# Strassen-like feed-forward tiles: the raw weight blocks fetched from ScalarE's queue instead of GpSimd's

## The reference

```
def _swiglu(x, w_gate, w_up, w_down):
    return (jax.nn.silu(x @ w_gate) * (x @ w_up)) @ w_down
```

## Time and profile before

| | before |
|---|---|
| median of 3 runs | 2195.53 us |
| profiled execution | 2196.21 us |
| its span | 2194.5 us |
| PE busy | 2070.7 us (94%) |
| DVE, ACT, POOL busy | 1491.7, 1085.4, 936.0 us |
| TensorE clock granted, mean | 0.991 of full speed |
| GpSimd's queue of transfers | 20096 packets, 72.18 MB |
| ScalarE's queue | 11712 packets, 27.27 MB |
| SP's queue | 51120 packets, 182.08 MB |

### The profile page before, as it was taken

The page is one execution under the profiler, slowest core; times in us unless marked ns, Lnnn a source line. Parts: engine busy times, 40 slices in busy tenths (PEclk is TensorE's granted clock), DMA queues, the critical chain, the costliest instruction groups (busy, mean ns, idle before and its releaser), DMA issues.

```text
span 2194.5 us, 34752 instructions
## 1 busy us (share of the span) xinstructions
PE 2070.7 (94%) x11738; PEld 1799.7 (82%) x11738; DVE 1491.7 (68%) x2525; ACT 1085.4 (49%) x1982; POOL 936.0 (43%) x709
## 2 busy tenths in 40 slices
PE   8999999898899989888999999999999998988998
PEld 6878888698888879888887788888878887988886
DVE  5597854787752378886258789899777348877523
ACT  4566653544442354444244476777655334444422
POOL 2233451755643275664327701201264317565431
PEclk9999999999999999999999999999999999999999
DMA  5322263455533244554325422222454434555321
GB/s 169 113 91 94 77 221 91 149 173 173 179 126 96 77 153 156 176 177 133 96 86 163 124 68 82 77 78 82 134 173 158 154 96 136 184 178 176 121 96 67
DMA packets 83026, 282.78 MB, mean 129 GB/s; under 512 B 9224, under 2 KB 9480, under 8 KB 82416
## 3 DMA queue, kind: packets, MB, share of 16 engines
q1 hardware_dynamic: 51120, 182.08, 26.5%
q0 software_dynamic: 20096, 72.18, 9.7%
q10 hardware_dynamic: 11712, 27.27, 3.3%
HBM read 261.03 MB, written 18.89 MB: 128 GB/s over the span
## 4 chain that ended last, share of the span: by engine, by line
PE 56%; issue 15%; DVE 12%; POOL 11%; ACT 2%; DMA 2%; POOLq 1%; SPq 0%; DVEq 0%; ACTq 0%
PE bank L188 15%; PE bank L190 15%; PE bank L189 15%; PE bank L195 2%; PE bank L194 2%; DMA w_raw<-stream 2%; DVE w_lo L162 2%; POOL s_raw L809 2%; POOL s_holes L812 2%; POOL s_raw L810 2%; POOL s_raw L812 2%; POOL s_holes L809 1%; PE bank L2218 1%; POOL s_holes L810 1%; DVE t_lo L666 1%
## 5 line engine op out<-in xcount | busy, mean ns | idle before, releaser
L162 DVE TENSOR_TENSOR w_lo<-w_raw,w_hi 128x1024 fp32r<-128x1024 f32 (+1 forms) x337 | 455.6, 1367 | 335.5 <-ACT w_hi L157 332.8
L157 ACT ACTIVATE w_hi<-w_raw 128x1024 fp32r<-128x1024 f32 (+1 forms) x337 | 331.2, 985 | 391.0 <-PE bank L190 233.0
L188 PE MATMUL bank<-xn_hi,w_hi 128*128 128x512 f32 (+1 forms) x1192 | 434.2, 364 | 7.5 <-DVE h L662 4.1
L190 PE MATMUL bank<-xn_hi,w_lo 128*128 128x512 f32 (+1 forms) x1192 | 419.8, 352 | 0.0
L189 PE MATMUL bank<-xn_lo,w_hi 128*128 128x512 f32 (+1 forms) x1192 | 418.8, 351 | 0.0
L188 PEld LDWEIGHTS bank<-xn_hi,w_hi 128*128 128x128 f32 x1192 | 226.1, 190 | 38.9 <-DVE h L662 5.4
L190 PEld LDWEIGHTS bank<-xn_hi,w_lo 128*128 128x128 f32 x1192 | 225.5, 189 | 31.0
L189 PEld LDWEIGHTS bank<-xn_lo,w_hi 128*128 128x128 f32 x1192 | 226.1, 190 | 28.2 <-issue 2.6
L843 POOL TENSOR_TENSOR down_lo<-h,down_hi 128x512 fp32r<-128x512 f32 x66 | 112.4, 1708 | 239.7 <-ACT down_hi L603 239.7
L188 PE MATMUL bank<-down_hi,w_hi 128*128 128x512 f32 x528 | 206.4, 391 | 6.3 <-POOL down_lo L843 6.3
L190 PE MATMUL bank<-down_hi,w_lo 128*128 128x512 f32 x528 | 206.2, 390 | 0.0
(11 more groups left out here) (488 smaller groups left out, 4933.0 us busy)
## 6 DMA issues: line engine op xcount, KB each, us to landing
w_raw<-stream SPq DMA_DIRECT2D x337, 512.0 KB, 3.6
s_raw<-stream POOLq DMA_DIRECT2D x54, 512.0 KB, 4.6
s_holes<-stream POOLq DMA_DIRECT2D x48, 512.0 KB, 4.9
spill_g<-gate_out ACTq DMA_DIRECT2D x16, 256.0 KB, 2.0
m_more<-spill_g POOLq DMA_DIRECT2D x3, 1024.0 KB, 11.1
s_first<-stream POOLq DMA_DIRECT2D x6, 512.0 KB, 4.3
x<-xt SPq DMA_DIRECT2D x4, 512.0 KB, 7.3
x<-xt ACTq DMA_DIRECT2D x1, 2048.0 KB, 9.7
```

The lines of the kernel that those rows point to most:

```text
L157: nc.scalar.activation(w_hi[:, slot, at], w_raw[:, slot % 2, at], ACT.Copy).then_inc(split_hi, 1)
L162: nc.vector.tensor_tensor(w_lo[:, slot, at], w_raw[:, slot % 2, at], w_hi[:, slot, at], ALU.subtract).then_inc(split_lo, 1)
L188: nc.tensor.matmul(to, a_hi, b_hi, start=start, stop=False, skip_group_check=True)
L190: return nc.tensor.matmul(to, a_lo, b_hi, start=False, stop=stop, skip_group_check=True)
```

## The change

The raw fetches move from GpSimd's list to ScalarE's. The first one stands after the root of the norm, the second in the third plain tile. Then `third_raw` stands ahead of the first `seven` and behind each `seven` up to the 15th: it waits for the fourth low part of the tile after this one, and issues the two transfers of the tile three ahead into the same buffer. GpSimd's `sums` wait for a landing and nothing else. The transfers count on two semaphores of their own. The loop of ScalarE ends one pass earlier, and that pass is written out. What the transfers carry, their sizes, their buffers and all sums and low parts stay as they were.

```diff
+        raw_in = x_in[2:]
...
+            def raw_to(eng, i, q):
+                for g in range(2):
+                    chunk = stream[4 * i + (first_in + gate_of(q) + g)]
+                    if q == 0 or (isinstance(i, int) and i == 0):
+                        to = (s_raw if q == 0 else s_first)[:, g].rearrange("p h w -> p (h w)")
+                        eng.dma_start(to, chunk).then_inc(raw_in[q], 16)
+                    else:
+                        eng.dma_start(s_holes[g][:, :, H:S], chunk.rearrange("p (k c) -> p k c", c=H)
+                                      ).then_inc(raw_in[q], 16)
...
                                      scale=1.0 / D).then_inc(m["root"], 1)
+                raw_to(act, 0, 0)
...
+                def third_raw(i, q):
+                    of, to = {-1: ((i, 0), (i + 1, 0)), 0: ((i, 1), (i + 1, 1)), 1: ((i + 1, 0), (i + 2, 0))}[q]
+                    act.wait_ge(c["lo"], part_made("lo", *of, 4))
+                    raw_to(act, *to)
...
+                    if t == 2:
+                        raw_to(act, 0, 1)
                     silu_of(t % 2, 2 * t + 2 * b + 1)
+                third_raw(0, -1)
                 for q in range(2):
                     seven(0, q, True)
-                with act.Fori(1, BODIES - 1) as i:
+                    third_raw(0, q)
+                with act.Fori(1, BODIES - 2) as i:
                     for q in range(2):
                         seven(i, q, True)
+                        third_raw(i, q)
+                for q in range(2):
+                    seven(BODIES - 2, q, True)
+                    if q == 0:
+                        third_raw(BODIES - 2, q)
...
-                def next_raw(i, q):
-                    pool.wait_ge(c["lo"], part_made("lo", i, q, 4))
-                    raw_to(i + 1, q)
-
                 def sums(i, q):
-                    pool.wait_ge(gates_in[q], 32 * i + (raw_loaded[q] + 32))
+                    pool.wait_ge(raw_in[q], 32 * i + (raw_loaded + 32))
...
-                raw_to(0, 1)
-                sums(0, 0)
-                sums(0, 1)
-                finished(pool, first_in, 2 * PLAIN - 1)
-                for q in range(2):
-                    next_raw(0, q)
-                    sums(1, q)
-                with pool.Fori(1, BODIES - 1) as i:
+                for i in range(2):
                     for q in range(2):
-                        next_raw(i, q)
-                        sums(i + 1, q)
+                        sums(i, q)
+                with pool.Fori(2, BODIES) as i:
+                    for q in range(2):
+                        sums(i, q)
```

## The result

The changed kernel takes 2251.84 us (median of four runs, 2250.97 to 2254.33), the kernel before 2195.61 beside it: a ratio of 1.0258, 95% interval 1.0241 to 1.0276. The change makes the kernel 56 us slower. I had forecast slower, by 18.7 us, and the range ended at 2240. The profiled run of the change took 2250.97 us.

The account below looks back on a forecast made before the run. GpSimd's ring of issue, landing and sums was taken to pace the kernel at 11.76 us a tile. A new ring of 12.25 gave 606.5 against 587.8, +18.7 on 2196.2, less 0.7: 2214 us, range 2150 to 2240.

Parts of the forecast that it names:

- (1): GpSimd in the loop: issuing and waiting, 5.06 us per tile, leave it; four sums remain, so it is no bound.
- (2): ScalarE's wait for S3's low part stands ahead of snap 0, which TensorE's S2 block needs; that closes a new ring.
- the 10.4: Length in us of a tile in the new ring without any hindrance from GpSimd's sums, 0.3 over the matmuls.
- Step (3): In the loop GpSimd's sums and vector operations take turns: a tile is L + 7.27, 12.25 us in the mean, against 11.76.
- step (5): Ahead of the loop: GpSimd's first sums come earlier, ScalarE's second fetch late; taken as zero, bounds -2 and +2 per feed-forward.
- L: Time from the end of S3's low part until the fetched blocks are there: 4.7 us for s_raw, 5.2 for s_holes.
- The turn of 0.42: Time in us added when a GpSimd sum and a two-operand vector operation exclude each other; three counted per tile.
- Step (4): The count: 15 tiles of 12.25 plus 18.4 for the last two intervals, 202.2 per feed-forward; +18.7 us over three.
- The ring goes and nothing takes its place: Rival: GpSimd's ring leaves the loop and no sum is in the way; 10.4 us a tile, 2136 us; chance 0.27 with its half-hindered case.
- its half-hindered case: Rival's variant: half the turns fall into the vector engine's idle time; 11.2 us a tile, 2169 us; within the shared 0.27.
- The tie: Rival: quicker landing (L = 4.3) or luckier turns make old and new rings equal; 11.75 us a tile, 2192 us; chance 0.16.
- The slow queue: Rival: transfers are slower on ScalarE's queue, L = 5.5; 12.8 us a tile, 2239 us; chance 0.12.

Follow-up runs that it names:

- small sums: The changed kernel with each of GpSimd's four sums on 16 of 512 columns; 2141.31 us, ratio 0.9755.
- the wait in the kernel before: The kernel before with only ScalarE's wait for S3's low part added behind each silu, GpSimd still issuing; 2229.91 us, ratio 1.0136.
- the wait kept at the old place: The changed kernel with ScalarE's issues moved behind snap 0 of the next tile, its wait also kept ahead of the weights' high part; 2247.92 us.
- s_raw's single transfer: The changed kernel with the two transfers of each even tile (s_raw) made one of 1024 KB; 2243.58 us, ratio 1.0222.

## Why the prediction came out as it did

**The mechanism was right.** Steps (1) and (2): GpSimd is busy 87.5 of 194 us of the loop (below) and bounds nothing; snap 0 behind S3's low part closes a ring, and TensorE's largest wait is the one forecast, 2.1 us for snap 0. The price of that ring without turns was low: ScalarE needs 1.70 us (573.81 to 575.51) or 1.52 (586.93 to 588.45) before the high part, where I put 0.95. That turns the 10.4 into 11.1, what the small sums measured.

**Step (3) failed in size.** 12.25 us a tile predicted, 13.13 measured in the first feed-forward (441.79 to 638.68, 15 intervals); 0.88 x 45 = 40 us, of a miss of 38; the last two intervals added 1 and step (5), below, gave back 5; the last 2 are the rounding of the forecast and the median against the profiled run. Each tile splits at its first sum, at L. Means over the first feed-forward:

| | predicted | measured |
|---|---|---|
| L, block in s_raw | 4.7 | 5.15 (4.83 to 5.31) |
| L, block in s_holes | 5.2 | 5.94 (5.80 to 6.27) |
| from the first sum on | 7.27 | 7.28 to 7.30 where the turns go as walked; 7.55 in the mean |

L is 0.62 longer, 28 of the 40 us. The queue isn't slower. Issues of the stretch 485 to 640, answering to the earlier trace rows (count, KB, median us from issue to landing):

```profile
s_holes<-stream ACTq DMA_DIRECT2D x12, 512.0 KB, 4.6
s_raw<-stream ACTq DMA_DIRECT2D x10, 512.0 KB, 4.0
```

They were 4.7 and 4.2 on GpSimd's queue. The Trainium skill's 0.4 us earlier first byte for a hardware queue (DMA: Bandwidth & Descriptors, Specifications) shows here as 0.1 to 0.2. But each of these medians mixes the first and the second transfer of a pair, and the sums wait for the second. One pair of s_holes, the first and the second issue alone, after (issued at 574.01 and 574.75) and before (588.52 and 589.31):

```profile
s_holes<-stream ACTq DMA_DIRECT2D x1, 512.0 KB, 4.2
s_holes<-stream ACTq DMA_DIRECT2D x1, 512.0 KB, 4.8
...
s_holes<-stream POOLq DMA_DIRECT2D x1, 512.0 KB, 4.3
s_holes<-stream POOLq DMA_DIRECT2D x1, 512.0 KB, 4.9
```

Over the first feed-forward of the change the second transfer lands 5.0 us after its issue for s_holes and 4.4 for s_raw, where I took 4.7 and 4.2. The parts of L in one tile of each, with what I had taken:

| | predicted, holes / raw | 573.81, s_holes | 586.93, s_raw |
|---|---|---|---|
| end of the low part to the first issue | 0 | 0.20 | 0.20 |
| first issue to the second | 0.5 | 0.74 | 0.53 |
| second issue to its landing | 4.7 / 4.2 | 4.83 | 4.41 |
| landing to the first sum | 0 | 0.07 | 0.06 |
| L | 5.2 / 4.7 | 5.84 | 5.20 |

In the means over the first feed-forward the second's landing makes 0.24 of the excess, the way from the low part to the issue 0.17, the issues 0.12 and the way to the sum 0.07. I had taken an issue from another transfer, 0.44; one of s_holes takes 0.56 (above). The earlier trace rows held the better number: 5.06 us from the first issue to the first sum for s_raw, and 5.00 in the change (587.13 to 592.13).

The turn of 0.42 holds: where no operation slips, 4 x 1.28 + 3 x 0.42 + 0.89 gives 7.27, and 7.28 was measured. The whole-instruction price of the Trainium skill (SBUF — State Buffer, "Who interferes with whom"), a turn of about 0.6 by my estimate, would have given 7.8, and here the measurement decides against that price; an L821 that took turns lasted 1.74 and an L823 1.62, 0.46 and 0.34 over a sum alone.

Most of the other 0.28 goes with TensorE's clock, of which I had said nothing. Granted clock in windows of the change: a tile, another, the steady loop, and one part of the first tile.

```profile
507.90:521.20 13.30, 10.59 (x77) 10.38 (x76) 9.28 (x15) 5.44 (x10) 5.46 (x4) 0.87 0.46 158
586.93:599.57 12.64, 10.03 (x84) 9.83 (x83) 9.89 (x14) 5.44 (x10) 5.79 (x4) 1.00 0.47 166
442.00:636.00 194.00, 164.14 (x1245) 161.08 (x1244) 139.10 (x191) 81.04 (x149) 87.53 (x60) 0.93 0.48 162
510.50:513.50 3.00, 2.69 (x12) 2.69 (x13) 2.43 (x3) 1.57 (x4) 0.46 (x1) 0.50 0.75 266
```

The same of the kernel before:

```profile
442.60:636.70 194.10, 176.42 (x1422) 171.67 (x1421) 153.15 (x219) 91.40 (x166) 110.22 (x90) 1.00 0.52 173
```

Before, it was 1.00 in this stretch. In the change the clock is at its lower level, 1.2 GHz (0.50), for a part of 20 of the 45 ring tiles. TensorE stands for snap 0 ahead of S2 for up to 3.2 us: for 2.2 us or more in 18 of these 20, and in 7 of the 25 tiles in which the clock stayed up. The other kernels with a full ring show it too (0.94 in the same stretch of the wait in the kernel before, 0.96 with the wait kept at the old place), the faster ones hardly (0.99 behind snap 2 and with small sums). What it costs: of the tiles of s_raw, 13 with the clock low took 13.17 us in the mean and 8 without 12.59; of s_holes 7 took 13.48 and 17 took 13.26. 13 x 0.58 + 7 x 0.22 = 9 us, an estimate. How, two tiles of the change show, both fetching to s_raw (TensorE's first matmuls of S2, the second low part, the second and third sum):

```profile
510.81 0.58 PE L189 MATMUL bank<-t_hi,s_hi 128*128 128x256 f32 x1 [2.71 <-ACT snaps L568]
...
514.28 1.30 POOL L821 TENSOR_TENSOR s_raw<-s_raw 128x512 f32<-128x512 f32 x1
...
515.66 1.29 POOL L823 TENSOR_TENSOR s_raw<-s_raw 128x512 f32<-128x512 f32 x1
515.68 1.82 DVE L695 TENSOR_TENSOR s_lo<-s_holes,s_hi 128x512 fp32r<-128x512 f32 x1
...
593.45 1.78 DVE L695 TENSOR_TENSOR s_lo<-s_holes,s_hi 128x512 fp32r<-128x512 f32 x1
...
594.76 1.61 POOL L823 TENSOR_TENSOR s_raw<-s_raw 128x512 f32<-128x512 f32 x1
```

In the first the low part comes 7.78 us behind the start of its tile (515.68 - 507.90), two sums are done by then and the third starts ahead of it (at 515.66); in the second it comes at 6.52 (593.45 - 586.93). The slow tile ends 8.16 us behind its first sum, the other 7.44. With s_raw's single transfer the first low part of such a tile comes 3.6 to 3.9 us behind its start, for 4.0 to 4.4 in the change, and the tiles of s_raw with the clock low take only 7.40 to 7.45 from the first sum on (7.50 to 8.52 in the change). The part behind the first sum is 9.6 us shorter over the 21 tiles of s_raw, and that is where that kernel's 8 us come from. That the clock falls because of the standing is not shown, only that the two go together; no kernel was run that stands as long with the clock held up.

**Step (4)** was right in its form: 18.8 us for the last two intervals (18.4 predicted), and the joint feed-forward, 215.6, no worse than the others. **Step (5)**, zero with bounds of 2 each, was -0.8, -2.7 and -1.9.

**The rivals.** "The ring goes and nothing takes its place" was wrong for this change, but its pace exists: with the fetch behind snap 2 the 45 tiles take 11.2 in the mean, the 11.2 of its half-hindered case, and the kernel 2165 beside 2169. The tie was wrong. The slow queue came nearest in time (L = 5.5, 2239; the mean L was 5.57) for a cause that didn't happen: the same blocks land on ScalarE's queue as early as on GpSimd's or earlier. So what failed is the sum for L in step (3): I took the median of all transfers for the second of a pair, which lands 0.2 to 0.3 later, took its issue from a transfer of another shape, and put the way from the low part to the issue and from the landing to the sum at nothing. The 9 us that go with the clock were no term of the sum at all.

## What to carry to other kernels

A wait for a free buffer, put into an engine that works in order, holds back everything behind it: list what stands there and who waits for it, and move the refill behind the last operation that the bounding engine wants. Here that choice alone, for the same fetch, lies between 2252 us (ahead of snap 0), 2210 (behind it) and 2165 (behind snap 2). When a way through a transfer is part of a ring, count the signal, every issue ahead and the way from the landing to its reader as well (1.0 us of 5.84 here), and take the landing of the transfer that the reader waits for, not a median over all. Some 1.4 us of that way decided between 56 us and nothing.

## What the hardware did that I had not expected

- Issues of the same 512 KB on ScalarE's queue took unlike times: 1.30 us for the two of s_holes, 0.87 for the two of s_raw.
- The same s_holes transfers went in smaller packets on ScalarE's queue. GpSimd's queue has 15552 packets less than before, 144 for each of the 108 transfers; ScalarE's has 33984 more, and the page counts 24576 more packets under 2 KB, which is 512 for each of the 48 transfers of s_holes. They landed no later for it.
- TensorE's clock was at its lower level in a part of 20 of 45 tiles of a loop in which it stood up to 3.2 us in a tile of 13, and stood at 1.00, 1.00 and 0.99 in the three loops of the kernel before.
- The same kernel, the one before with the wait alone, took between 2219.71 and 2252.16 over five executions, and in one of them the joint feed-forward took 201.9 us and the other two 219.0 and 219.5.
